# Three block borders of a four-layer decoder trunk: x is turned in parts, the chunks whose columns are final first, and the next block's first products are interleaved with the turns

## The reference

```
for i in range(4):
    h = rms_norm(x, norm_mix[i]);  x = x + mixer_i(h)     # stick-breaking, S5, MLA, stick-breaking
    h = rms_norm(x, norm_ffn[i]);  x = x + ffn_i(h)       # dense SwiGLU on i = 0, 2; 2 of 8 experts on i = 1, 3
return rms_norm(x, final_norm)
```

## Time and profile before

| | |
|---|---|
| runs, median (lowest to highest) | 1736.39 us (1732.41 to 1738.27) |
| profiled execution, its span | 1734.57 us, 1732.9 us |
| PE busy | 1668.0 us, 96% of the span |
| DVE, ACT, POOL busy | 1293.6, 1002.6, 220.3 us (75%, 58%, 13%) |
| chain that ended last | PE 73%, DVE 12%, ACT 6% of the span |

### The profile page before, as it was taken

How to read it: one execution, slowest core, us unless ns; L and a number is a source line. 1 busy time by engine, 2 the same in 40 slices (tenths; PEclk the granted TensorE clock), 3 DMA queues, 4 the chain that set the end, 5 groups by cost and what they waited for, 6 DMA issues and landing times.

```text
span 1732.9 us, 26753 instructions
## 1 busy us (share of the span) xinstructions
PE 1668.0 (96%) x11011; PEld 1545.0 (89%) x11011; DVE 1293.6 (75%) x1283; ACT 1002.6 (58%) x920; POOL 220.3 (13%) x230
## 2 busy tenths in 40 slices
PE   6999999989999999999989999999999999999996
PEld 6999999779899999999779999998998999999995
DVE  4578998785789888888867555446548888888886
ACT  5565333343576777777645443335557777777773
POOL 4407992010000000000210000000000000000011
PEclk9999999989999999999999999999999999999998
DMA  7427887575389899999942254454334999999993
GB/s 287 144 110 261 266 307 247 205 281 189 140 326 375 342 370 358 374 354 359 363 150 106 74 218 182 146 186 168 113 142 180 364 353 349 373 349 368 358 383 150
DMA packets 53482, 449.28 MB, mean 259 GB/s; under 512 B 6736, under 2 KB 8944, under 8 KB 16640
## 3 DMA queue, kind: packets, MB, share of 16 engines
q1 hardware_dynamic: 48480, 430.40, 66.0%
q0 software_dynamic: 4896, 17.35, 2.8%
HBM read 426.63 MB, written 21.10 MB: 258 GB/s over the span
## 4 chain that ended last, share of the span: by engine, by line
PE 73%; DVE 12%; ACT 6%; issue 4%; DMA 3%; POOL 1%; POOLq 0%; DVEq 0%; ACTq 0%; SPq 0%
PE PS L323 21%; PE PS L325 21%; PE PS L324 21%; DVE wlo L375 5%; ACT whi L368 3%; DMA yg<-expert_rows,offi 1%; DMA expert_rows<-ysb 1%; PE PS L2084 1%; PE PS L2047 1%; PE PS L2048 1%; PE PS L1722 1%; PE PS L495 1%; PE PS L896 1%; DVE x L2314 1%; DMA raw<-in_weights 1%
## 5 line engine op out<-in xcount | busy, mean ns | idle before, releaser
L375 DVE TENSOR_TENSOR wlo<-raw,whi 128x3072 fp32r<-128x3072 f32 (+1 forms) x278 | 854.9, 3078 | 186.7 <-ACT whi L368 185.8
L368 ACT ACTIVATE whi<-raw 128x3072 fp32r<-128x3072 f32 (+1 forms) x278 | 705.9, 2541 | 330.1 <-PE PS L325 305.0
L323 PE MATMUL PS<-wlo,hT_hi 128*128 128x384 f32 (+3 forms) x1840 | 594.2, 323 | 1.9 <-DVE wlo L375 1.4
L325 PE MATMUL PS<-whi,hT_hi 128*128 128x384 f32 (+3 forms) x1840 | 591.0, 321 | 0.0
L324 PE MATMUL PS<-whi,hT_lo 128*128 128x384 f32 (+3 forms) x1840 | 591.0, 321 | 0.0
L323 PEld LDWEIGHTS PS<-wlo,hT_hi 128*128 128x128 f32 x1840 | 347.2, 189 | 6.1 <-DVE wlo L375 1.7
L324 PEld LDWEIGHTS PS<-whi,hT_lo 128*128 128x128 f32 x1840 | 347.3, 189 | 2.9
L325 PEld LDWEIGHTS PS<-whi,hT_hi 128*128 128x128 f32 x1840 | 347.1, 189 | 0.3
L323 PE MATMUL PS<-wlo,mhi 128*128 128x512 f32 x352 | 143.5, 408 | 0.8 <-DVE mlo L2338 0.8
L324 PE MATMUL PS<-whi,mlo 128*128 128x512 f32 x352 | 139.1, 395 | 0.0
L325 PE MATMUL PS<-whi,mhi 128*128 128x512 f32 x352 | 139.1, 395 | 0.0
(11 more groups left out here) (394 smaller groups left out, 2051.1 us busy)
## 6 DMA issues: line engine op xcount, KB each, us to landing
raw<-in_weights SPq DMA_DIRECT2D x203, 1536.0 KB, 8.1
raw<-in_weights SPq DMA_DIRECT2D x73, 1024.0 KB, 7.1
raw<-s_tables SPq DMA_DIRECT2D x8, 1536.0 KB, 7.2
expert_rows<-ysb POOLq DMA_DIRECT2D x14, 512.0 KB, 9.6
s_tables<-g_out SPq DMA_DIRECT2D x8, 640.0 KB, 3.5
t_af<-s_rows_af SPq DMA_DIRECT2D x32, 128.0 KB, 3.8
s_tables<-g_out SPq DMA_DIRECT2D x8, 512.0 KB, 3.7
raw<-in_weights SPq DMA_DIRECT2D x3, 1152.0 KB, 11.1
```

The source lines that it names most:

```text
L323: pe.matmul(o, sh, mlw, start=start, stop=False, skip_group_check=True)
L325: return pe.matmul(o, sh, mh, start=False, stop=stop, skip_group_check=True)
L368: act.activation(whi[p0 % SPL][:, 0:n], raw[p0 % RAW][:, 0:n], ACT.Copy).then_inc(hi_done, 1)
L375: dve.tensor_tensor(wlo[p0 % SPL][:, 0:n], raw[p0 % RAW][:, 0:n], whi[p0 % SPL][:, 0:n].bitcast(F32), ALU.subtract).then_inc(lo_done, 1)
```

## The change

At the three borders PE turns x in parts:

- Border 1 and 5: chunks 0 to 3 are turned in the middle of the last projection product (third slice, second row tile, between its contraction chunks 3 and 4), behind a new wait on `x_early`, which DVE raises once the adds of the first two slices are done. Chunks 4 and 5 follow behind that product, and 6 and 7 between the products of chunks 3 and 4 in the dense block's first piece.
- Border 6: chunks 0 to 3 are turned ahead of the last of the four tiles of the down projection, behind `x_early`, raised after the adds of the first half. Chunks 4 to 7 follow behind the first 12 matmuls of sb1.
- DVE writes `hT_lo` of chunks 0 to 3 directly behind `x_early`, ahead of the last adds. At borders 1 and 5 it splits the first held-back piece between chunks 5 and 6.
- `CHUNK_AT` puts the early chunks into banks that the projection has left.

ACT's program is not changed: `hT_hi` of all 8 chunks still stands ahead of the squares.

```diff
@@ late_turns @@
-            turn_x(pe, n, range(KC))
+            turn_x(pe, n, range(4, KC) if n == 6 else (6, 7))
...
         def proj_pe(pe, b0, ready, n):
...
+                        if (i, t) == (2, 1) and k == KC // 2:
+                            pe.wait_ge(x_early, EARLY[n])
+                            turn_x(pe, n, range(4))
...
+            turn_x(pe, n, (4, 5))
...
-                if i < len(DCOLS) - 2:
-                    split_lo(dve, b0 + i + SPL)
+                if i == 0:
+                    split_lo(dve, b0 + SPL)
+                elif i == 1:
+                    ins.then_inc(x_early, 1)
+                    hT_low(dve, n, range(4))
...
@@ norm_dve @@
+                if n in (1, 5):
+                    hT_low(dve, n, (4, 5))
+                    split_lo(dve, base[STAGES[n]] + SPL - 2)
+                    hT_low(dve, n, (6, 7))
+                    mean_sq(dve, n)
+                    split_lo(dve, base[STAGES[n]] + SPL - 1)
+                    return
@@ gate_or_up in dense_pe, first piece @@
-                        if k == 0:
+                        if k == 4:
                             late_turns(pe, n)
@@ first_columns of sb1 @@
+                hT_ready(pe, norm, 3)
+                part(0, range(4))
                 late_turns(pe, norm)
-                hT_ready(pe, norm, 3)
-                for c in range(3):
+                for c in range(1, 3):
                     part(c, range(4))
@@ last_down in dense_pe @@
+                    if (f, i, half, t) == (1, JD - 1, 1, 1):
+                        pe.wait_ge(x_early, EARLY[6])
+                        turn_x(pe, 6, range(4))
@@ the adds behind a dense block @@
+                if f == 1 and half == 0:
+                    i.then_inc(x_early, 1)
+                    hT_low(dve, 6, range(4))
```

More of the change, by code:

```diff
@@ L307, in hybrid_trunk @@
         gain_in = sem("gain_in")
-        x_up, x_most, p_half = sem("x_up"), sem("x_most"), sem("p_half")
+        x_up, x_most, p_half, x_early = sem("x_up"), sem("x_most"), sem("p_half"), sem("x_early")
         first_hi, first_lo = sem("first_hi"), sem("first_lo")
@@ L463, in hybrid_trunk @@
         TP0, HI0, LO0, SQ0 = ([sum(c[:n]) for n in range(9)] for c in (TURNS, HIS, LOS, SQS))
-        AFTER_PROJ = ((6, 0), (7, 0), (2, 0), (3, 0), (4, 0), (5, 0), (6, 1), (7, 1))
+        EARLY = {1: 1, 5: 2, 6: 3}
         CHUNK_AT = {0: ((0, 0), (1, 0), (2, 0), (3, 0), (7, 0), (4, 0), (5, 0), (6, 0)),
-                    1: AFTER_PROJ, 5: AFTER_PROJ,
[2 rows of a table added]
                     4: ((4, 0), (5, 0), (6, 0), (7, 0), (2, 0), (3, 0), (4, 1), (5, 1)),
@@ L584, in mean_last, with hT_low @@
                                      in1=stat[:, 1, t:t + 1], op0=ALU.mult, op1=ALU.add).then_inc(nrm_ms, 1)
+        def hT_low(dve, n, ks):
+            for k in ks:
+                dve.wait_ge(nrm_hi, HI0[n] + k + 1)
+                dve.scalar_tensor_tensor(out=hT_lo[:, k, :], in0=chunk(n, k), scalar=gain_of(n, k),
+                                         in1=hT_hi[:, k, :].bitcast(F32), op0=ALU.mult, op1=ALU.subtract)\
+                    .then_inc(nrm_lo, 1)
         def norm_dve(dve, n):
@@ L592, in norm_dve @@
             if n not in WHOLE:
[L593 to L597, removed]
+                if n in (1, 5):
[5 more added lines that the diff above has]
+                    return
+                hT_low(dve, n, range(4 if n == 6 else 0, KC))
                 if n == 0:
@@ L688, in proj_pe, with proj_dve @@
                 last.then_inc(w_used, 1)
-        def proj_dve(dve, b0, banks):
+            turn_x(pe, n, (4, 5))
+        def proj_dve(dve, b0, banks, n):
             for i, (c0, w) in enumerate(DCOLS):
@@ L927, in out_tile @@
                 for k in ks:
-                    if a == 1 and (i, t) == (2, 1) and k == KC // 2:
-                        pe.wait_ge(x_most, 2)
-                        turn_x(pe, 7, range(6))
+                    if (i, t) == (2, 1) and k == KC // 2:
+                        if a == 0:
+                            pe.wait_ge(x_early, EARLY[1])
+                            turn_x(pe, 1, range(4))
+                        else:
+                            pe.wait_ge(x_most, 2)
+                            turn_x(pe, 7, range(6))
                     oh, ol = o_parts(a, k)
@@ L1006, in sb_pe @@
                 out_tile(2, 1, range(KC)).then_inc(w_used, 1)
+                turn_x(pe, 1, (4, 5))
             else:
@@ L1223, in sb_dve @@
                     s5_turns_dve(dve, part)
-                proj_dve(dve, b0 + 9, SB_BANKS)
+                proj_dve(dve, b0 + 9, SB_BANKS, n + 1)
             else:
@@ L2896, in mla_dve @@
             CHAIN_V[0] = k[0]
-            proj_dve(dve, b0 + 6, ((0, 1), (2, 3), (4, 5)))
+            proj_dve(dve, b0 + 6, ((0, 1), (2, 3), (4, 5)), 5)
         block = ctx.enter_context(nc.Block())
```

## The result

The changed kernel takes 1739.40 us (median of 20 runs, 1736.14 to 1743.24), the kernel before 1734.36 us (20 runs, 1730.73 to 1740.81). The ratio is 1.0024, interval [1.0016, 1.0033]: slower by 4.2 us (2.8 to 5.7), under the 0.3% that were set as telling a change from none. The forecast was +5.1 us and 1740.5.

What follows compares the result with a forecast made beforehand. PE was taken as the bound, busy 1668.0 of 1732.9 us. Terms -1.4 (border 5), +3.4 (border 1) and +3.1 (border 6) sum to +5.1: 1739.7 from the profiled run, 1741.5 from the median, named 1740.5, range 1731 to 1745.

Steps and rivals of the forecast that it cites:

- the clock at border 6: Border 6: the clock falls behind PE's 2.5 us wait at sb1's second piece, costing 1.7 us more.
- Border 5, -1.4: Border 5: DVE is free and nothing waits, so PE's gap shrinks to the transposes, -1.4 us.
- Border 1, `x_early`: Border 1: PE waits 2.8 us instead of 2.09; the dense block starts at 147.7, before at 146.97.
- Border 1, ACT's line, +3.4: Border 1: ACT's squares and splits queue behind the last `hT_hi`, so PE resumes at `act` 3.4 us later.
- The power of 0.56 us rather than 3.59: Border 1: POOL's second power takes 0.56 us, since DVE waits then; with 3.59 the sum would be 6.1.
- Border 6, +1.4: Border 6: the chain hangs on the last `hT_hi`; sb1's second piece comes 1.4 us later, PE waits 2.5 us.
- the window near 0.6: Border 6: sign of the forecast, a clock window near 0.6 with the wait ahead of sb1's second piece.
- from about 1.85 us of waiting on: PE's waits: the length from which the clock was taken to fall, about 1.85 us.
- gaps alone: Borders 1 and 6: ACT's later squares are covered after all; -1.6 to -3.3 us, 1733.0 to 1731.3; chance 0.17.
- the clock holds: New waits at borders 1 and 6: no fall at one or both; +3.4 or +1.7 us; chance 0.18.
- the third fall: Border 6: the clock already drops at sb1's start, delaying the whole chain; +6.5 us; chance 0.15.

Runs made afterwards that it cites:

- e1_no_b1: The changed kernel with border 1 taken back to the kernel before, borders 5 and 6 still changed: 1734.85 us, ratio 0.9999 to the kernel before.
- e3_act_b6: The changed kernel with ACT's `split_hi` of sb1's piece 1 moved between the fourth and fifth `hT_hi` at border 6: 1735.98 us, ratio 1.0009 to before.
- e4_act_all: e3_act_b6 with ACT's squares also moved between the sixth and seventh `hT_hi` at borders 1 and 5: 1731.43 us, ratio 0.9978 to before.
- e5_warm1: e4_act_all with three spare matmuls on PE in its wait for `x_early` at border 1: 1731.77 us, ratio 0.9980 to before.
- e6_warm2: e5_warm1 with three more spare matmuls in PE's wait for `act` in dense block 0: 1730.10 us, ratio 0.9974 to before.
- e9_best: e4_act_all, piece 2's `split_hi` and DVE's means ahead of the last two `hT_hi`/`hT_lo` (borders 1, 5), spare matmuls before `x_early` (border 1) and `act`: 1729.77 us.
- e10_best_k: e9_best with two more spare matmuls ahead of attention's wait for `kT` in sb0: 1730.15 us, ratio 0.9982 to before.
- e11_before_warm: The kernel before with two spare matmuls in each of its waits, for x at border 1 and for `act`: 1732.79 us, ratio 0.9993.

## Why the prediction was right

It named the direction, the size and the places. All its steps were met but one term, the clock at border 6, so that part of how near 5.1 comes to the measured 4.2 is luck: with that term at nothing the sum would be 3.4, which is as near. By its steps:

- **Border 5, -1.4:** B changed by -1.49.
- **Border 1, `x_early`:** forecast a wait of 2.8 us and a start of the dense block at 147.7; measured 2.70, and 149.39 - 1.97 = 147.4. (The working let PE arrive 1.25 us ahead of the end of the tile. That is 11 matmuls at 0.113 us; twelve are 1.36, a slip of 0.1 us.)
- **Border 1, ACT's line, +3.4:** A changed by +3.05. The wait for `act` was put at 4.5 us (by the working's own terms, 1.85 + 3.4 - 0.9, it is 4.35) and is 4.27. The power of 0.56 us rather than 3.59 was right; the sum with 3.59 would have been 1 us further off.
- **Border 6, +1.4:** C changed by +1.32, the wait forecast at 2.5 us is 2.50. The steps inside hold too: 1.2 us were forecast at `x_early`, and 1.1 lie between the end of PE's third tile and the turns; sb1 was to start 1.4 us earlier, and starts 1.40 earlier as counted from the first add.
- **Border 6, clock, +1.7:** this term was wrong as stated, and the window near 0.6 that was to show it is 1.00. The sum took it for certain because the clock had fallen behind 2.09 and 1.85 us. It held here and fell in e1_no_b1, with the same code and the same wait.

The three distances sum to +2.9 us, the runs say +4.2 (2.8 to 5.7). One fall at half clock lowers the mean granted clock of an execution by 1.7 / 1740 = 0.001, and that of the changed kernel's 20 runs is lower by 0.0011 than that of before (0.9870 against 0.9881). So an execution of it has about one fall more, which can be the missing 1.3 us. Whether it comes at border 6 or elsewhere is not shown, as these runs have no traces, and the chips are not the same.

The trace of before alone speaks against that step. It holds this row and its window:

```profile
42.23 0.71 PE L881 MATMUL PS<-qT,kT 64*128 64x256 f32 x4 [2.16 <-DVE kT L1123]
```

```profile
42.00:46.00 4.00, 3.77 (x26) 3.68 (x27) 3.35 (x2) 2.84 (x5) 0.00 (x0) 1.00 0.81 266
```

A wait of 2.16 us, the granted clock 1.00 behind it. The working used only the waits behind which the clock fell, and its "from about 1.85 us of waiting on" does not stand: besides this one, waits of 1.76 to 2.77 us for `act` and of 2.73 us at border 1 left the clock at 1.00 in four of the later profiles. The same wait for kT in the profile of the changed kernel is longer, and the clock fell behind it:

```profile
42.57 1.15 PE L900 MATMUL PS<-qT,kT 64*128 64x256 f32 x4 [3.39 <-DVE kT L1147]
```

Of the rivals, "gaps alone" failed on A and C, "the clock holds" was what this profile shows at border 6, and the third fall did not come. That the cause is the order in ACT's queue was argued before and is shown by e3_act_b6 and e4_act_all: ACT's instructions were the same, only moved. At border 6 that turned the loss into a gain (C 16.80, then 14.14; before 15.48). At border 1 it took half of the loss back (A 52.60, then 51.09; before 49.55).

## What to carry to other kernels

When work is released in parts, look at every engine whose queue holds something urgent behind the last part: here ACT's squares and splits stood behind the eighth `hT_hi`, and turning the last chunks late delayed all of them by the length of PE's detour. Moved into the idle time that the split opens between the parts, the same instructions gave back 1.5 us at border 1 and 2.7 us at border 6, together 4.2 us of the 4.4 that the change had lost at the two. Compare distances between landmarks inside the traces where medians don't resolve 1 us, read the mean granted clock of every run beside its time (0.001 less of it went with 0.7 to 1.2 us here), and charge a clock fall behind a wait of 2 to 3 us as a chance, not as a certainty.

## What the runs showed of the hardware

The clock of TensorE falls to 1.2 GHz behind some waits and not others of the same length. Behind PE's wait at border 1 (2.1 to 2.7 us, no spare matmul) it fell in seven profiles of eight; behind the wait for `act` between 1.76 and 2.79 us in two of six, and in all three of 4.3 us; behind the 2.5 us at border 6 in one of two. Behind the wait for kT at 42 us it held in all three profiles with 2.16 to 2.38 us and fell in all nine with 2.63 to 3.51. One fall on the chain cost 1.54 us (A of e4_act_all against e5_warm1). In the nine places where spare matmuls filled the wait (one in e5_warm1, two each in e6_warm2, e9_best, e10_best_k and e11_before_warm) it stayed at 1.00. Where two of them came only after 2.13 us of waiting (e10_best_k, kT) it fell.
